# Expert blocks of 128 rows with one expert, or of two 64-row halves with an expert each and a second accumulator

## The reference

```
h = LayerNorm(alpha * x + mixers(x))
y = LayerNorm(alpha * h + HierMoE(h))
# HierMoE: 4 groups of 8 experts; a token takes the best group, then its top 2 experts in it
#   run_block: (silu(xb @ w_eg[e]) * (xb @ w_eu[e])) @ w_ed[e]      # 1024 -> 256 -> 1024
#   y_a = ys[dest] * gate;  out = zeros.at[tok].add(y_a)
```

## Time and profile before

| | us |
|---|---|
| median of 3 runs | 3192.64 (3190.05 to 3194.82) |
| profiled execution, its span | 3185.8 |
| mixer and attention | 0 to 2078 |
| router | 2078 to 2383 |
| dispatch | 2383 to 2420 |
| experts: first gather to first gate product | 2421 to 2430 |
| experts: gate(0) to the end of down(63) | 2430.0 to 3113.4 |
| experts: last result and its adds | 3113.4 to 3129.5 |
| combine | 3129.5 to 3185.8 |

### The profile page before, as it was taken

One profiled execution on the slowest core, in us unless ns is written; L12 is line 12 of the kernel. 1 busy time (PEld: TensorE's weight loads), 2 busy tenths in 40 slices (PEclk: granted clock), 3 DMA queues, 4 the chain that ended last, 5 costly groups with the idle time before them and its releaser, 6 DMA issues. The chain is left out here.

```text
span 3185.8 us, 65923 instructions
## 1 busy us (share of the span) xinstructions
PE 2883.6 (91%) x26600; PEld 2202.1 (69%) x26600; DVE 1738.2 (55%) x3821; ACT 970.2 (30%) x2497; POOL 522.3 (16%) x554
## 2 busy tenths in 40 slices
PE   7999999999999999669899898989976999999990
PEld 6888888888888888545555555545545777777770
DVE  1666666666666666558686868822235222222225
ACT  2333333333333333234343434412220111111116
POOL 0000000000000000010000000011113554545540
PEclk9999999999999999689999999999988999999995
DMA  6211111222111211420101010033335899886447
GB/s 196 37 38 37 37 37 38 40 39 39 37 38 39 42 38 37 93 88 1 39 1 39 1 36 1 1 127 132 126 110 210 282 336 325 278 279 177 97 93 251
DMA packets 337225, 310.23 MB, mean 97 GB/s; under 512 B 235200, under 2 KB 290528, under 8 KB 322528
## 3 DMA queue, kind: packets, MB, share of 16 engines
q1 hardware_dynamic: 315424, 238.88, 24.5%
q0 software_dynamic: 21504, 67.13, 9.1%
HBM read 208.12 MB, written 84.42 MB: 92 GB/s over the span
## 5 line engine op out<-in xcount | busy, mean ns | idle before, releaser
L814 PE MATMUL mx_bank<-mx_xT,mx_w_in 128*128 128x128 f32 x5168 | 646.4, 281 | 16.9 <-DVEq L281 13.4
L814 PEld LDWEIGHTS mx_bank<-mx_xT,mx_w_in 128*128 128x128 f32 x5168 | 600.8, 193 | 60.5 <-issue 36.2
L2311 DVE STREAM_TRANSPOSE ex_xT<-ex_x 128x256 f32<-128x256 f32 x256 | 141.5, 610 | 332.3 <-DMA ex_x<-scr_hx,ex_idx 332.3
L1497 PE MATMUL at_bank<-pl_kT,pl_qT 128*128 128x512 f32 (+5 forms) x656 | 289.9, 528 | 2.3 <-issue 2.3
L1469 ACT ACTIVATE at_PQ<-at_bank,at_nms 128x512 f32<-128x512 f32 (+5 forms) x328 | 192.7, 595 | 252.9 <-DVE at_nms L1597 251.5
L2159 POOL DMA_INDIRECT ex_x<-scr_hx,ex_idx x256 | 244.9, 957 | 114.8 <-issue 77.7
L2242 PE MATMUL ex_gate<-pl_wg,ex_xT 128*128 x1024 | 233.6, 381 | 13.7 <-DVE ex_xT L2311 11.4
L2242 PEld LDWEIGHTS ex_gate<-pl_wg,ex_xT 128*128 128x128 f32 x1024 | 195.1, 191 | 68.7 <-issue 44.9
L2266 PE MATMUL ex_down<-pl_wd,ex_hT 128*128 x512 | 230.3, 592 | 1.5 <-ACT ex_hT L2194 1.5
L2242 PE MATMUL ex_up<-pl_wu,ex_xT 128*128 x1024 | 231.6, 379 | 0.0
L1528 PEld LDWEIGHTS at_bank<-at_PT,at_vals 128*64 128x64 f32 (+1 forms) x2208 | 117.4, 136 | 151.5 <-issue 78.1
(11 more groups left out here) (310 smaller groups left out, 4480.2 us busy)
## 6 DMA issues: line engine op xcount, KB each, us to landing
pl_wg<-in_w_eg SPq DMA_DIRECT2D x32, 1024.0 KB, 6.1
pl_wu<-in_w_eu SPq DMA_DIRECT2D x32, 1024.0 KB, 10.3
pl_wd<-in_w_ed SPq DMA_DIRECT2D x32, 1024.0 KB, 14.3
mx_x<-in_x SPq DMA_DIRECT2D x76, 128.0 KB, 3.7
pl_ro_x<-in_x SPq DMA_DIRECT2D x17, 512.0 KB, 4.2
scr_hx<-ro_h SPq DMA_DIRECT2D x17, 512.0 KB, 2.6
scr_acc<-ro_ha SPq DMA_DIRECT2D x17, 512.0 KB, 3.1
co_r<-scr_acc SPq DMA_DIRECT2D x17, 512.0 KB, 5.6
```

The costliest lines, as they stand in the source:

```text
L814: ins = pe.matmul(dst, w_in[:, k, col:col + n], xT[:, k, :], start=(k == 0), stop=(k == KC - 1))
L1497: t.mark(pe.matmul(bank[n % SB][:, 0:wd], qT[h][keys(h), j * P:(j + 1) * P], kT[h][keys(h), k0 * P:k0 * P + wd], start=True, stop=True), f ...
L2311: ins = v.transpose(xT[s][:, :, 32 * h:32 * h + 32], x[s][:, h, :].rearrange("p (i k) -> p k i", k=KC))
```

## The change

Blocks are still 128 rows wide, but are made of two halves of 64 rows, each half with an expert of its own; `NBLK` becomes 48 (96 halves). In each block:

- Gate, up and down are issued as pairs of products with 64 stationary columns: the left half with the weights in the expert's slot into PSUM partitions 0 to 63, the right half into partitions 64 to 127 with the weights in three extra buffers `bg`, `bu`, `bd`.
- VectorE copies the right half's gate and up weights (128x2048 each) from their slot to `bg` and `bu`, ScalarE the down weights to `bd`, for every block. Each reads the expert's rank from a table into a register first.
- The turn of `hid` is 4 ordinary products with 64 stationary columns in place of 2 transposes.
- GpSimd issues the gathers of block i+2 ahead of add(i).
- The weights are loaded in the order in which experts appear; gate and up of an expert when the up product of its predecessor's last block is done, down when the down product is done. In dispatch the first loads wait for VectorE's count of the used experts.
- A token's rows in right halves are added to a second accumulator, which the router clears tile by tile, and combine loads both and adds them, GpSimd columns 0 to 511 and VectorE the rest.

```diff
-NBLK = (ASSIGN + NE * (P - 1)) // P
+HB = P // 2
+NSUB = (ASSIGN + NE * (HB - 1)) // HB
+NBLK = NSUB // 2
@@ router
+                blank_out.go(sp.dma_start(second[col, :], blank[:]))
@@ dispatch
+            sp.wait_ge(first_used, 1)
             for s in range(SLOTS):
-                sp.sem_inc(weights.w_in[s].sem, 16 * weights.w_in[s].n)
-                load_expert(sp, io, weights, s, bass.ds(s, 1))
+                e = bass.ds(sp.value_load(keep["free_at"][0:1, s:s + 1], min_val=0, max_val=NE - 1), 1)
+                load_expert_in(sp, io, weights, s, e)
+                load_expert_out(sp, io, weights, s, e)
...
-            do(v.tensor_tensor(cmp1[:], bc(counts, KB), bm(nums[:, 0:KB], NE), ALU.is_gt))
-            do(v.tensor_reduce(blocks[:], cmp1[:], AX.X, ALU.add))
+            do(v.tensor_scalar(blocks[:], counts, 1.0 / HB, 0.5 - 0.5 / HB, ALU.mult, ALU.add))
+            rounded(blocks[:])
+            do(v.tensor_scalar(live[:], blocks[:], 1.0, None, ALU.min))
             do(v.tensor_tensor_scan(ends[:], ones[:, 0:NE], blocks[:], 0.0, ALU.mult, ALU.add))
+            do(v.tensor_tensor_scan(seen[:], ones[:, 0:NE], live[:], 0.0, ALU.mult, ALU.add))
...
@@ experts, SP
+            for r in range(NE):
+                if r >= SLOTS:
+                    e = bass.ds(sp.value_load(keep["free_at"][0:1, r:r + 1], min_val=0, max_val=NE - 1), 1)
+                    groups = sp.value_load(groups_of[0:1, r - SLOTS:r - SLOTS + 1], min_val=1, max_val=NBLK)
+                    sp.wait_ge(up_done, groups)
+                    load_expert_in(sp, io, given, r % SLOTS, e)
...
+                if r >= SLOTS:
+                    sp.wait_ge(down_done, groups)
+                    load_expert_out(sp, io, given, r % SLOTS, e)
@@ experts, GpSimd
+            def add(i):
+                s = i % 2
+                if i > 0:
+                    g.wait_ge(y_add[1 - s].sem, y_add[1 - s].done((i - 1) // 2))
+                g.wait_ge(y_made, i + 1)
...
             for i in range(2):
+                gathers(i)
+            for i in range(NBLK):
+                if i + 2 < NBLK:
+                    gathers(i + 2)
+                add(i)
@@ experts, ScalarE (per block: tanh, turned and result of the block before, then)
+            def second_out(i):
+                e = rank(a, 2 * i + 1)
+                at = slot(a, e)
+                a.wait_ge(out_ready, a.snap(e + 1))
+                a.activation(bd[:], flat(wd[:, at, :]), ACT.Copy).then_inc(bd_made, 1)
@@ experts, TensorE (gate(i), turned(i-1), up(i), down(i-1) as before)
+                for k in range(KC):
+                    c = slice(k * FE, (k + 1) * FE)
+                    pe.matmul(out[s][0:HB, 0:FE], xT[s][:, k, 0:HB], wv[:, c], start=(k == 0), stop=(k == KC - 1))
+                    ins = pe.matmul(out[s][HB:P, 0:FE], xT[s][:, k, HB:P], b[:, c], start=(k == 0), stop=(k == KC - 1))
...
+            def gate(i, e, at):
+                pe.wait_ge(xT_made, i + 1)
+                pe.wait_ge(in_ready, pe.snap(e + 1))
+                pe.wait_ge(bg_made, i + 1)
...
                 for m in range(FC):
-                    ins = pe.transpose(turn_b[s][:, m * P:(m + 1) * P], hid[s][:, m:FE:FC], ident[:, :])
+                    for half in range(2):
+                        f = slice(half * HB * FC + m, (half + 1) * HB * FC, FC)
+                        ins = pe.matmul(turn_b[s][half * HB:(half + 1) * HB, m * P:(m + 1) * P], hid[s][:, f], ident[:, :],
+                                        start=True, stop=True)
@@ experts, VectorE
+            def second_gate(i):
+                e = rank(v, 2 * i + 1)
+                at = slot(v, e)
+                v.wait_ge(in_ready, v.snap(e + 1))
+                if i > 0:
+                    v.wait_ge(gate_done, i)
+                v.tensor_copy(bg[:], flat(wg[:, at, :])).then_inc(bg_made, 1)
+                return at
+            def second_up(i, at):
+                if i > 0:
+                    v.wait_ge(up_done, i)
+                v.tensor_copy(bu[:], flat(wu[:, at, :])).then_inc(bu_made, 1)
...
+            for i in range(NBLK):
+                more = i + 1 < NBLK
                 if more:
+                    turned(i + 1)
+                silu(i)
+                if more:
+                    at = second_gate(i + 1)
+                hidden(i)
+                if more:
+                    second_up(i + 1, at)
@@ combine
                 sp.dma_start(r[t % NB][:], scr["acc"][t * P:(t + 1) * P, :]).then_inc(r_in[t % NB], 16)
+                sp.dma_start(c[t % NB][:], scr["acc"][TOK + P + t * P:TOK + P + (t + 1) * P, :]).then_inc(c_in[t % NB], 16)
...
+                g.tensor_tensor(r[k][:, 0:LOW], r[k][:, 0:LOW], c[k][:, 0:LOW], ALU.add).then_inc(low_summed, 1)
...
+                v.tensor_tensor(r[k][:, LOW:D], r[k][:, LOW:D], c[k][:, LOW:D], ALU.add).then_inc(high_summed, 1)
```

More of the change, by code:

```diff
@@ L1985, in _ @@
             ins.then_inc(counted, 1)
+            pe.wait_ge(columns, 1)
+            for k in range(3):
+                ins = pe.matmul(turned[0:32, k * P:(k + 1) * P], bcol[:, k, :], ident, start=True, stop=True)
+            ins.then_inc(turns, 1)
             for k, (n0, n1) in enumerate(PARTS):
@@ new lines, in _ @@
+            do(v.tensor_scalar(over[:], last_rank[:], own, float(NSUB), ALU.is_le, ALU.mult))
+            do(v.scalar_tensor_tensor(out=past[:], in0=ends[:], scalar=own, in1=live[:], op0=ALU.is_le, op1=ALU.mult))
+            do(v.tensor_reduce(bcol[:, 0, 0:1], past[:], AX.X, ALU.add))
+            do(v.tensor_scalar(bcol[:, 0, 0:1], bcol[:, 0, 0:1], last_rank[:, 0:1], None, ALU.min))
+            do(v.tensor_scalar(past[:], seen[:], own, None, ALU.is_le))
+            do(v.tensor_reduce(bcol[:, 1, 0:1], past[:], AX.X, ALU.add))
@@ L2284, in _ @@
-            at = slot(e)
-            gate(t, 0, e, at)
-            up(t, 0, at)
-            second_half(t, u)
-            for i in range(1, turns):
-                t, u, past = Turn(pe, ten, i), Turn(pe, down, i), Turn(pe, down, i - 1)
-                e = expert(i * 2)
-                at, at1 = slot(e), slot(expert(i * 2 - 1))
-                gate(t, 0, e, at)
-                turned(past, 1)
-                hten.whole()
-                up(t, 0, at)
-                result(past, 1, at1)
-                down.whole()
-                second_half(t, u)
@@ L2306, in _, with turned @@
+                ins.then_inc(down_done, 1)
+            before = None
+            for i in range(NBLK):
+                e = rank(pe, 2 * i)
+                at = slot(pe, e)
+                gate(i, e, at)
+                if i > 0:
+                    turned(i - 1)
+                up(i, at)
+                if i > 0:
+                    down(i - 1, *before)
+                before = e, at
+            turned(NBLK - 1)
+            down(NBLK - 1, *before)
         @block.vector
         def _(v):
-            def turned(t, s):
-                t.arrived(x_in[s])
+            def turned(i):
+                s = i % 2
+                v.wait_ge(x_in[s].sem, x_in[s].done(i // 2))
+                if i >= 2:
+                    v.wait_ge(up_done, i - 1)
```

375 lines of the change are left out of this document (178 added, 197 removed).

## The result

The changed kernel takes 3272.4 us (median of 4 runs, 3247.1 to 3291.5) against 3191.4 (3190.1 to 3194.8): 1.025 times the time before, 95% interval 1.020 to 1.030. I had forecast 3181. Its runs spread over 44 us where those before spread over 5.

The account below looks back on a forecast made before the run. TensorE was taken to bound the experts stage before, a GpSimd-ordered chain after; experts -42.8, dispatch +1.6, first weights +5, combine +24 sum to -12.2, span 3173.6, plus 6.8 carried over: 3181 us, range 3130 to 3245.

Parts of the forecast that it names:

- TensorE's part: Experts stage: two half products cost what one full product does; with the turn, a block needs 10.78 us of TensorE.
- The chain: From the end of down(b-2) over result, add, gathers, transposes and weight copy to gate(b); sets a period of 13.54 us.
- rival 4: TensorE bounds the experts stage instead of the chain: stage 519 us, total 3059; chance 0.05.
- L: Time from the last gather's issue until transposes can start: taken as 3.2 us, 1.64 for blocks without tokens.
- rival 1: Loads keep gathers as long as before, mean L 5.4 us: +43, total 3224; chance 0.17.
- E: TensorE's time for one block, 10.78 us; with X it gives the period T = (X + E) / 2.
- at 0.91, + 24: TensorE's granted clock falling to 0.91 while it idles: E 11.85, +24 us, held only in the range.
- rival 2: VectorE's weight copies hold up GpSimd's add and gathers, one 1.35 us copy entering the chain: +31, total 3212; chance 0.17.
- X: Chain from the end of down(b-2) to gate(b): 13.1 + L, so 16.3 us, or 14.74 without tokens.
- `bu`, `bd`, weights: Experts stage: `bu` and `bd` copies hidden; SP's new waits cost 0, as loads run some 3.8 blocks ahead.
- Dispatch and router: Ahead of the experts stage: dispatch's VectorE operations +1.6 us, router's clearing 0; first weights issued later, +5.
- Combine: Last stage: DMA engines bound it; 17 more tiles cost 22 us, the first tile's second load and addition 2: +24.

Follow-up runs that it names:

- e1: Changed kernel with gathers one block further ahead: blocks 0 to 2 first, then gathers(i+3) in front of add(i); 3079.1 us, 0.965 of the kernel before.
- e6: Kernel before with only GpSimd's order changed: two blocks of gathers first, then gathers(b+2) in front of add(b); 3371.5 us, 1.058 of the kernel before.
- e13: Changed kernel with SP issuing the next gate and up load before its wait for down and the previous expert's down load; 3257.2 us, 1.021 of before.
- e2: Changed kernel, experts after the first four loading only 64 of 2048 weight columns; 3192.9 us, stage 655.0 against 734.9.
- e11: Changed kernel with SP's expert load also waiting until the next block's gathered rows are transposed; 3230.3 us, 1.013 of the kernel before.
- e5: Changed kernel with idle TensorE products ahead of every second block's gate, half as many as in an earlier try; 3251.8 us, stage 710.1 against 734.9.
- e4: Changed kernel with the copies of the right half's gate and up weights on ScalarE instead of VectorE; 3235.8 us, 1.014 of the kernel before.
- e7: Changed kernel, combine loading only 64 of 1024 columns of the second accumulator's tiles from tile 5 on; 3269.4 us, 1.025 of before.
- e8: Changed kernel, combine loading both accumulators in full but not adding the second; 3254.8 us, 1.023 of the kernel before.

## Why the prediction was wrong

The direction was wrong with the mechanism right. By its own steps:

- **TensorE's part, right.** Pairs overlap: up takes 3.46, and a warm block 10.8 to 10.9. e1's period of 10.77 is the 10.78 of the working.
- **The chain, right in kind.** Every second gate waits for `bg`; the links that no load or copy touches came as worked out (result to add 2.1, the copy 1.22 against 1.35). e6 and e1 show that the lost block of cover makes it. What I had of it as a price was too low: 122 us in the working (640.6 against the 519 of rival 4), and 196 measured, since it turned a gain of 144 us (683.4 to 539.1 in e1) into a loss of 51.
- **L, the step that failed first.** "Now gate's and up's weights, two thirds of it, are issued at the end of up, 3.43 us earlier." The trace shows 19 of the 28 issued 1.6 to 2.1 us behind the down load of the expert before, 17 of them as close behind the end of a down product (the expectation of e13 gives the 19 for that; 17 is right). SP's queue is in order, and its wait for down stood in front of them; I had listed the next expert's load as standing behind that wait and costed it at nothing, since weights have three experts of lead. They do. It was the gathers that paid. In the working with L = 1.64 throughout the stage is 610, with loads 640.6: 30 for the loads. e2 measured 80. These 50 us are rival 1 (43 for a mean L of 5.4): over the 21 waiting chains that lead from gate(4) to gate(47), L is 5.4 on average in place of my 3.2 and 1.64, which makes 52 us. e11 shows where the loads stand to be worth some 42, e13 the order alone about 15. And e13 shows a second fault in the step: with the loads at the end of up, as I had assumed, L of the waiting gates is still 5.2 in blocks 3 to 27. The loads' issue moved 4.9 us forward, L fell by 1.9 (one profile each).
- **E behind a wait, the second step that failed, and about as large.** The clock stood only in the range ("at 0.91, + 24"), although the sum itself had TensorE idle 2.8 us in 13.5. A gate behind a wait of 2.6 to 13 us took 5.0 to 6.6 us instead of 3.6, in 24 blocks (block 3, behind 3.2 us, took 3.7). In the same chains E is above 10.78 by 46 us in all. e5, which fills the waits in part, takes some 25 off the stage. The mean clock of 0.89 was near the 0.91 of the range, but the loss lies in the gates that waited, each of which counts in full.
- **The copies' hold on GpSimd,** rival 2: real, but not on the chain. In blocks without loads nearly every second group of gathers took 5.4 to 5.7 in place of 4.7, and it goes with the copies (e4). But it is the group of the block whose gate doesn't wait, and there the time is hidden under TensorE. In the chains that set the period the four gathers took 4.7 us. So next to nothing of the 31 us of rival 2 was paid. The rule of the Trainium skill (SBUF — State Buffer, SBUF: two separate sides) held: with VectorE's copies between SBUF tiles, the issue of 0.95 became 2.69. The 45 us that e2 leaves are the slow gates (nearly 40) and the two ends of the stage.
- **Rivals as exclusive cases.** I gave a chance to each case alone and none to their sum, though loads and clock lengthen the same chain. Forecast, + 43, + 24 and + 31 give 3279, near the measured 3272, but that is chance: the 31 was not paid, and the other two came dearer. Against the 94.3 us of the stage, L makes + 52 and the slow gates + 46; the other links of X were 7 us shorter than worked out, one X fewer lies in the measured path (- 6), gate(4) came 6.6 late and the last turn took 3.5 more. A wait shows without loads too (e2), so the clock's cost comes from the chain itself.
- **`bu`, `bd`, weights.** Right: up never waited, down 3.1 us once, and SP's waits left no gate waiting for weights but one, for 2.6 us.
- **Dispatch and router.** Dispatch, from its first instruction to the first gather, +1.0 against +1.6; the router's stretch is 1.2 longer in these two profiles (309.7 to 311.2 in all 16) against 0. The first gather starts at 2420.9 and 2421.1, but gate(0) is 20.3 us behind it in place of 9.1: +11.2 against +5, because the unit matrix, which gate(0) had not had to wait for before (1.7 us on its way), came behind 12.6 MB of weights.
- **Combine,** +23.7 against +24, right by luck, for the wrong reason. I had the DMA engines as its bound; e7 and e8 show VectorE, with three passes that GpSimd's additions lengthen, and the DMA engines 0.25 us a tile behind.

## What to carry to other kernels

Count the cover of an in-order queue in turns of the bounding engine before and after an edit: gathers one block nearer to their use cost 188 us in the kernel before (e6) and 193 in the changed one (e1), though each looked like a reordering of two lines. Where an edit makes a chain, add up everything that can lengthen it (loads in front of its transfers, the clock behind its waits), for such cases come together and not in each other's place. And look in which blocks a delay falls: here nearly all the long gathers were those of blocks whose gate did not wait, and cost nothing. A wait in a DMA queue costs not only the late load, but also moves every load behind it, into the transfers of others.
